# A fused two-model forward pass on one core: the layer norms without their filler matmuls

## What is computed

```python
def layer_norm(x, g, b):
    mu = jnp.mean(xf, axis=-1, keepdims=True)
    var = jnp.mean(jnp.square(xf - mu), axis=-1, keepdims=True)
    return (xf - mu) * lax.rsqrt(var + LN_EPS) * g + b

for layer in range(DEPTH):
    x = layer_norm(ALPHA * x + 0.5 * swiglu(x, ...), ...)
    mix = rglru_block(x, ...) if layer < N_A else dilated_attention(x, k_shared, v_shared, ...)
    x = layer_norm(ALPHA * x + mix, ...)
    x = layer_norm(ALPHA * x + 0.5 * swiglu(x, ...), ...)
```

## Time and profile before

| | us |
|---|---|
| three runs, median (lowest to highest) | 1805.95 (1804.25 to 1807.08) |
| profiled execution, time | 1804.63 |
| its span | 1802.8 |
| TensorE busy | 1764.2 (98%) |
| TensorE weight loads | 1600.3 (89%) |
| VectorE busy | 1290.2 (72%) |
| ScalarE busy | 977.2 (54%) |
| filler matmuls (L579), 198 | 35.8 |
| mean granted TensorE clock | 0.988 |

### The profile page before, as it was taken

How to read it: one execution, slowest core, us unless ns; L and a number is a source line. 1 busy time by engine, 2 the same in 40 slices (tenths; PEclk the granted TensorE clock), 3 DMA queues, 4 the chain that set the end, 5 groups by cost and what they waited for, 6 DMA issues and landing times.

```text
span 1802.8 us, 33249 instructions
## 1 busy us (share of the span) xinstructions
PE 1764.2 (98%) x11768; PEld 1600.3 (89%) x11768; DVE 1290.2 (72%) x2099; ACT 977.2 (54%) x1708; POOL 0.2 (0%) x4
## 2 busy tenths in 40 slices
PE   9999999999999999999999998999999999999998
PEld 7888998888899888888788887889999998898887
DVE  6777789777665776778787766868655568787765
ACT  5564695656355554455465544565534355565543
POOL 0000000000000000000000000000000000000000
PEclk9999999999999999999999999999999999999999
DMA  7665465456545566422356663334455533346562
GB/s 223 189 200 192 127 198 170 149 187 206 180 142 176 189 194 201 138 89 100 104 202 187 196 196 111 117 112 135 140 175 193 181 118 118 112 134 198 186 204 88
DMA packets 76637, 290.77 MB, mean 161 GB/s; under 512 B 9344, under 2 KB 11648, under 8 KB 76544
## 3 DMA queue, kind: packets, MB, share of 16 engines
q1 hardware_dynamic: 76544, 289.50, 50.5%
HBM read 288.42 MB, written 1.05 MB: 161 GB/s over the span
## 4 chain that ended last, share of the span: by engine, by line
PE 91%; DVE 5%; ACT 2%; issue 1%; DMA 0%; SPq 0%; ACTq 0%; DVEq 0%
PE psum L500 33%; PE psum L501 17%; PE psum L492 11%; PE psum L494 11%; PE psum L493 11%; DVE wlo L1508 1%; PE psum L632 1%; PE psum L738 1%; PE psum L627 1%; DVE r L1680 1%; PE psum L579 1%; PE psum L737 1%; ACT whi L1043 1%; PE psum L860 1%; PE psum L867 1%
## 5 line engine op out<-in xcount | busy, mean ns | idle before, releaser
L1508 DVE TENSOR_TENSOR wlo<-raw,whi 128x1024 fp32r<-128x1024 f32 (+3 forms) x496 | 644.8, 1309 | 245.9 <-ACT whi L1043 245.1
L500 PE MATMUL psum<-x_split,whi 128*128 128x512 f32 x1760 | 618.4, 395 | 3.6 <-DVE x_split L1543 2.1
L1043 ACT ACTIVATE whi<-raw 128x1024 fp32r<-128x1024 f32 (+3 forms) x496 | 548.7, 1119 | 40.4 <-PE psum L494 21.5
L501 PE MATMUL psum<-x_split,wlo 128*128 128x256 f32 x1760 | 494.6, 281 | 0.0
L500 PEld LDWEIGHTS psum<-x_split,whi 128*128 128x128 f32 x1760 | 331.3, 188 | 81.8 <-DVE x_split L1543 2.5
L492 PE MATMUL psum<-x_split,whi 128*128 128x272 f32 (+1 forms) x1184 | 346.3, 293 | 4.6 <-DVE x_split L1716 3.4
L494 PE MATMUL psum<-x_split,wlo 128*128 128x272 f32 (+1 forms) x1184 | 338.6, 286 | 0.0
L493 PE MATMUL psum<-x_split,whi 128*128 128x272 f32 (+1 forms) x1184 | 337.7, 285 | 0.0
L501 PEld LDWEIGHTS psum<-x_split,wlo 128*128 128x128 f32 x1760 | 332.2, 189 | 0.0
L500 PE MATMUL psum<-h_split,whi 128*128 128x512 f32 x770 | 272.2, 397 | 0.0
L492 PEld LDWEIGHTS psum<-x_split,whi 128*128 128x128 f32 x1184 | 223.4, 189 | 14.9 <-issue 9.1
(11 more groups left out here) (231 smaller groups left out, 1769.8 us busy)
## 6 DMA issues: line engine op xcount, KB each, us to landing
raw<-w_in SPq DMA_DIRECT2D x264, 512.0 KB, 3.5
raw<-w_out SPq DMA_DIRECT2D x96, 704.0 KB, 4.4
raw<-w_mix SPq DMA_DIRECT2D x44, 512.0 KB, 3.6
raw<-w_rg SPq DMA_DIRECT2D x25, 512.0 KB, 4.1
raw<-w_q SPq DMA_DIRECT2D x24, 512.0 KB, 3.7
raw<-w_mixo SPq DMA_DIRECT2D x16, 576.0 KB, 3.7
raw<-w_kv SPq DMA_DIRECT2D x16, 512.0 KB, 3.7
raw<-w_rg_out SPq DMA_DIRECT2D x8, 640.0 KB, 3.9
```

Source lines behind the costliest of these rows:

```text
L500: nc.tensor.matmul(ps[:, bank, :], whi[slot][:, w], split, start=start, stop=False)
L501: return nc.tensor.matmul(part(bank, 0), wlo[slot][:, w], split[:, 0], start=False, stop=stop)
L1043: nc.scalar.activation(whi[slot][:, 0:cols], raw[slot][:, 0:cols], ACT.Copy).then_inc(w_hi_done, count)
L1508: V.tensor_tensor(wlo[slot][:, 0:cols], raw[slot][:, 0:cols], f(whi[slot][:, 0:cols]), ALU.subtract).then_inc(w_lo_done, 1)
```

## The change

The helper and its two calls in `layer_norm` of TensorE's stream are left out; nothing else is touched. 11 norms times 18, that is 198 matmuls with their 198 weight loads, are gone. What is computed is the same.

```diff
@@ -573,11 +573,6 @@
-        def keep_warm(count):
-
-            for _ in range(count):
-                nc.tensor.matmul(acc(7, SEQ), h_hi[:, 0, 0:P], h_hi[:, 0, 0:SEQ], start=True, stop=True)
-
@@ -655,13 +650,11 @@
                 pe.wait_ge(sq_done, KD * (n + 1))
                 ins = token_means(sq[:, KD - 1, :], 4, True)
             ins.then_inc(stat_done, 1)
-            keep_warm(6)
             pe.wait_ge(rstd_done, n + 1)
             for m, c in enumerate(starts):
                 ins = nc.tensor.matmul(ps[:, 6, c - starts[0]:c - starts[0] + P], rstd_t[:, m:m + 1].broadcast_to([P, P]),
                                        ident, start=True, stop=True)
             ins.then_inc(spread, 1)
-            keep_warm(12)
```

## The result

| | before | after |
|---|---|---|
| median of the runs, us (lowest to highest) | 1805.33 (1804.25 to 1807.08) | 1819.6 (1817.66 to 1820.61) |
| ratio, with its 95% interval | | 1.0077 (1.0062 to 1.0092) |
| span of the profiled execution, us | 1802.8 | 1817.1 |
| mean granted TensorE clock | 0.988 | 0.969 |
| TensorE busy, us | 1764.2 | 1754.1 |

What follows compares the result with a forecast made beforehand. TensorE was taken to bound the kernel, with 91% of the last-ending chain. 8.3 + 1.6 + 1.9 - 0.8 = 11.0 us gave 1815.6 us from the profiled execution, 1816.9 us from the median; 1816.0 us was taken, range 1808 to 1822 us.

Steps and rivals of the forecast that it cites:

- Eight norms, 8.3 us forecast: out0, rg_out, out1, out2, o, mixo0, out4, mixo1: first products at half clock for 4.3 us, each norm losing 1.04 us.
- the forecast's formula: First chunks, eight tiles: 4.3 us at half clock, remaining tiles at full clock, 7.59 us against 6.55 us paced by VectorE.
- half clock in the spreading (at nothing): Spreading of the reciprocal: 1.11 us against 0.71 us, taken as zero behind VectorE's centring; other end 0.4 us a norm.
- 1.6 us for its tiles and 1.9 us for its means, less 0.6 us: In emb: tiles 1.6 us and mean matmuls 1.9 us slower at half clock; reciprocal spread 0.6 us sooner.
- The 0.8 us saved at the spreading: Without the six first fillers the reciprocal is spread sooner: 0.6 us in emb, 0.2 us in mixo0, nothing in other norms.
- The overruns of the second fillers at nothing: Second fillers ending behind the first tile in mixo0, emb, out4, mixo1: removal gains zero, other end 3.0 us.
- (a): Rival: the clock does not fall without fillers; only 0.8 us gained, 1803.8 to 1805.2 us; chance 12%.
- (b): Rival: the clock falls in about half of the norms that kept it; 5 us, 1810 to 1811 us; chance 13%.
- (c): Rival: waits do not soften the loss, or half clock lasts about 6.6 us; 17 to 21 us slower; chance 8%.
- (d): Rival: faster, second fillers' overruns set the end and the clock stays up; 3.8 us, 1801 to 1802 us; chance 4%.

Runs made afterwards that it cites:

- thin fillers: All 198 fillers kept with their weight loads, each multiplying 2 columns instead of 256, against the kernel before: ratio 1.0092, 16.6 us slower.
- The last two of the faster kernels: Against the kernel before: 36 fillers added in emb, 16 and 18 around the recurrent block's output stage, ratio 0.9983; besides, 14 in each mixing stage, 0.9979.

## Why the prediction came out right, step by step

The direction and the mechanism held: slower, by the clock, in every norm. The forecast was 1816.0 us in a range of 1808 to 1822 us; measured were 1819.6 us. The loss in the profile is 14.3 us where the sum had 11.0 us, so the sum was some 3 us short, in the terms below. By its terms:

- **Eight norms, 8.3 us forecast.** Measured 9.5 us (the table without `emb`). The way to the price is confirmed: the first product is not late (but for `o`), TensorE's waits for VectorE go first, and only the rest is lost. With its real half-clock length put in, the forecast's formula gives 1.8, 1.1 and 0.7 us for `out0`, `out1` and `rg_out` (6.0, 4.5 and 3.6 us at half clock); measured are 1.68, 1.02 and 0.64 us, so it is too high by 0.1 us. The mis-sized term is the length: 4.3 us was taken from two stretches elsewhere, and it was 3.2 to 6.2 us, 4.6 us in the mean. With the real lengths the formula gives 9.5 us for the eight, to the tenth what was measured, but that is luck: it is 0.8 us too low in `o` and mostly some 0.1 us too high in the others.
- **`o`, in these 9.5 us with 1.82 us.** The step that was missing. I priced half clock in the spreading (at nothing) and not in the statistics. In `o` the clock had fallen behind them, and now it fell while they ran (918.2 us, 1.8 us after their start); the reciprocal was done 4.83 us after their start instead of 3.89 us: 0.94 us. The single-column matmuls show it, four of them grown from 0.59 to 0.99 us (the first row is from before, the others from after):

```profile
914.85 0.59 PE L632 MATMUL psum<-con,sq 128*128 128x1 f32 x4
...
918.63 0.85 PE L627 MATMUL psum<-con,r 128*128 128x1 f32 x4
919.34 0.99 PE L627 MATMUL psum<-con,sq 128*128 128x1 f32 x4
921.32 1.23 PE L655 MATMUL psum<-con,rstd_t 128*128 128x128 f32 x4 [0.98 <-DVE rstd_t L1691]
```

  The same cost stood already in the trace of before, in `mixo0`, where the clock fell among the statistics: six single-column matmuls took 1.42 us, and 0.81 us in the kernel with eighteen second fillers, which kept full clock there (second row). The reciprocal was done 5.40 us after the start of the statistics in the one and 4.71 us in the other: 0.7 us.

```profile
1257.07 1.42 PE L632 MATMUL psum<-con,sq 128*128 128x1 f32 x6
...
1257.25 0.81 PE L632 MATMUL psum<-con,sq 128*128 128x1 f32 x6
```

- **`emb`, 1.6 us for its tiles and 1.9 us for its means, less 0.6 us.** Measured: 1.86 us, 2.44 us, and 0.55 us saved net behind the reciprocal, together 3.75 us against the forecast's 2.9 us. The means ran at half clock for 5.0 us (until 1123.0) and took 6.40 us, where they took 3.95 us; I had 4.3 us at half clock and 5 to 6 us in all:

```profile
1118.02 6.40 PE L622 MATMUL psum<-r,con 128*128 128x272 f32 x16 [2.05 <-DVE r L1673]
...
1131.76 1.65 PE L655 MATMUL psum<-con,rstd_t 128*128 128x128 f32 x6 [0.56 <-DVE rstd_t L1691]
```

- **The 0.8 us saved at the spreading.** The prediction took the 0.16 us of waiting in `out0` for the delay of the signal. That wait counts from the end of the fillers; from the end of the reciprocal to the spreading it is 0.05 us (199.31 to 199.36 in the timeline of after, and 1131.71 to 1131.76 in `emb`), so by the forecast's own way the gain in `emb` and `mixo0` is 1.0 us rather than 0.8 us.
- **The overruns of the second fillers at nothing.** Confirmed by the kernel with eighteen of them, but for `emb`. Without fillers the first products of `mixo0`, `out4` and `mixo1` come 0.72, 0.33 and 0.48 us sooner than before, and the formula, which gives nothing for that, is not low there.
- **Outside the norms** the sum had nothing. The net is about 1 us (the start -1.65 us, the recurrent stage +0.96 us, a mixing stage +1.63 us).

Of the rivals, (a), that the clock does not fall, is out by the traces: it fell in all eleven norms. What the Trainium skill's rule on idle gaps ("TensorE: Matmul & The Clock Gate", "Why this matters for your kernels") would have protected did fall: with thin fillers TensorE's longest wait in the norm `out0` was 0.99 us, and the next products ran at half clock all the same. (b), that it falls in about half of the norms that kept it, is out for the kernel without any filler; of the kernels with a part of them, the one without the six first fillers is like it (two of five). (c), 17 to 21 us, is out too: 14.3 us were measured, with an interval up to 16.6 us. By the penalty that the Trainium skill gives for a half-rate stretch, half of its length ("TensorE: Matmul & The Clock Gate", Terms), 65 us more at half clock would cost 32 us, an estimate. The traces disagree for these stretches: in `out0`, 6.0 us of products at half clock would cost 2.7 us by their pace (0.214 against 0.117 us), and 1.68 us were lost, since waits for VectorE went away; and a part of the stretches was waiting. (d), faster, is out.

## What to carry to other kernels

When TensorE has to wait for statistics, read the granted clock over the wait and over the dense work behind it before calling fillers useless: they cost nothing where they end in time, and here they save 14 us in 1805. A filler must multiply enough columns; one that merely occupies the engine did nothing that could be measured. And price a half-clock stretch by what of the work in it is not paced by another engine: here it was 0.22 us for each microsecond, not the 0.45 us that dense products alone lose (0.214 us each against 0.117 us). Look at the statistics too: matmuls of one column also get slower at half clock, which put the reciprocal off by 0.9 us in `o` and 0.7 us in `mixo0`.

## What was not expected of the hardware

- Matmuls of 2 columns with their weight loads, which occupied TensorE for 1.48 us of a gap of 2.5 us, left the kernel as slow as with no work there at all, as far as the runs can tell (16.6 us slower, against 13.9 us; the intervals overlap).
- The clock may stay at half while TensorE is shown busy without a break: in `mixo0` of before, 6.60 of 6.6 us busy at 0.50, the work being statistics, fillers and the spreading.
- Where the clock falls is not settled by the code near it. The last two of the faster kernels are the same up to the first mixing stage, and yet one fell in `out1` (507.7 us) and the other did not; and runs of one kernel differ in their mean clock (0.980 to 0.988). What sets these places stays open; it moves a profile's sum by some 3 us.
